# Even input projection as four pairs of column tiles, each a two by two blocked product with seven products

## The reference

```python
D_MODEL = 1024; SEQ = 1024
EV_IN = 4608     # 2*512 (q, k of A) + 2*1024 (v, gate of A) + 3*512 (q, k, v of B)
def _even_mixer(x, positions, w_in, w_out):
    hproj = x @ w_in                                   # (1024 x 1024) @ (1024 x 4608)
    qa, ka, va, ga, qb, kb, vb = [hproj[..., offs[i]:offs[i + 1]] for i in range(len(sizes))]
    qa = _rotary(_heads(qa, RET_HEADS), positions, RET_DK, RET_THETA)
    ...                                                # retention and dilated attention
    return jnp.concatenate([ya, yb], -1) @ w_out
```

## Time and profile before

| | |
|---|---|
| median of three runs (lowest to highest) | 3026.54 us (3023.1 to 3028.83) |
| span of the profiled execution | 3027.1 us |
| TensorE, VectorE, ScalarE, GpSimd busy | 94%, 61%, 40%, 11% of the span |
| the projection: first to last matmul | 13.8 to 408.2 us |
| its matmuls | 1728 |
| first work of the next stage (VectorE, L1367) | 418.0 us |

### The profile page before, as it was taken

One profiled execution on the slowest core, in us unless ns is written; L12 is line 12 of the kernel. 1 busy time (PEld: TensorE's weight loads), 2 busy tenths in 40 slices (PEclk: granted clock), 3 DMA queues, 4 the chain that ended last, 5 costly groups with the idle time before them and its releaser, 6 DMA issues. The chain is left out here.

```text
span 3027.1 us, 45981 instructions
## 1 busy us (share of the span) xinstructions
PE 2850.5 (94%) x17614; PEld 2398.2 (79%) x17614; DVE 1856.5 (61%) x2964; ACT 1209.1 (40%) x2127; POOL 334.0 (11%) x273
## 2 busy tenths in 40 slices
PE   8999977988989999999989989799988999999998
PEld 6888866877878888788877877689977888887886
DVE  4111125683789999836379882255538899997365
ACT  3211125762354444422346752355433444443222
POOL 0000036330000000000000001355410000000000
PEclk9999988998989999999989999899998999999999
DMA  4222234335322222264422432532033222224444
GB/s 169 88 95 95 83 142 127 94 96 181 97 92 84 84 84 84 100 210 145 163 98 84 159 99 79 171 105 95 17 133 105 85 84 84 84 84 158 158 153 142
DMA packets 150493, 339.70 MB, mean 112 GB/s; under 512 B 35952, under 2 KB 69936, under 8 KB 139696
## 3 DMA queue, kind: packets, MB, share of 16 engines
q1 hardware_dynamic: 120128, 299.52, 28.9%
q10 hardware_dynamic: 30192, 37.82, 3.6%
HBM read 252.17 MB, written 85.10 MB: 111 GB/s over the span
## 5 line engine op out<-in xcount | busy, mean ns | idle before, releaser
L308 PE MATMUL even_in_acc<-even_in_w_hi,even_x_hi 128*128 128x512 f32 x576 | 225.5, 391 | 13.8 <-DVE even_x_lo L266 13.8
L272 DVE TENSOR_TENSOR even_in_w_lo<-even_in_w_raw,even_in_w_hi 128x512 fp32r<-128x512 f32 x72 | 49.6, 691 | 292.3 <-ACT even_in_w_hi L229 292.3
L309 PE MATMUL even_in_acc<-even_in_w_lo,even_x_hi 128*128 128x512 f32 x576 | 225.2, 391 | 0.0
L310 PE MATMUL even_in_acc<-even_in_w_hi,even_x_lo 128*128 128x512 f32 x576 | 225.2, 391 | 0.0
L1034 DVE TENSOR_TENSOR ffn_a_lo<-ffn_a_raw,ffn_a_hi 128x512 fp32r<-128x512 f32 x80 | 55.3, 691 | 217.5 <-ACT ffn_a_hi L936 217.5
L936 ACT CAST ffn_a_hi<-ffn_a_raw 128x512 fp32r<-128x512 f32 x80 | 49.8, 623 | 307.1 <-PE ffn_down_acc L980 277.6
L1128 POOL TENSOR_TENSOR ffn_down_rstd<-ffn_down_rstd,ffn_down_power 128x1 f32<-128x1 f32 x16 | 15.0, 939 | 1368.4 <-DVE ffn_down_rstd L1063 1368.4
L308 PEld LDWEIGHTS even_in_acc<-even_in_w_hi,even_x_hi 128*128 128x128 f32 x576 | 108.8, 189 | 36.3 <-issue 13.8
L310 PEld LDWEIGHTS even_in_acc<-even_in_w_hi,even_x_lo 128*128 128x128 f32 x576 | 108.7, 189 | 22.9
L309 PEld LDWEIGHTS even_in_acc<-even_in_w_lo,even_x_hi 128*128 128x128 f32 x576 | 108.8, 189 | 22.5
L980 PE MATMUL ffn_down_acc<-two_hi,ffn_a_hi 128*128 128x512 f32 x352 | 109.2, 391 | 4.4 <-DVEq L1028 2.6
(11 more groups left out here) (571 smaller groups left out, 8288.9 us busy)
## 6 DMA issues: line engine op xcount, KB each, us to landing
ffn_w_raw<-in_ffn_up SPq DMA_DIRECT2D x42, 1024.0 KB, 4.8
ffn_down_w_raw<-in_ffn_down SPq DMA_DIRECT2D x82, 512.0 KB, 3.6
ffn_a_raw<-hidden SPq DMA_DIRECT2D x86, 256.0 KB, 3.7
even_in_w_raw<-in_ev_w_in SPq DMA_DIRECT2D x18, 1024.0 KB, 5.7
hp<-even_in_stage ACTq DMA_DIRECT2D x18, 1024.0 KB, 4.4
even_out_w_raw<-in_ev_w_out SPq DMA_DIRECT2D x24, 512.0 KB, 3.6
hidden<-even_mixed SPq DMA_DIRECT2D x22, 512.0 KB, 2.6
ffn_w_raw<-in_od_w_qkv SPq DMA_DIRECT2D x11, 1024.0 KB, 5.7
```

The source lines that it names most:

```text
L272: dve.tensor_tensor(at(w_lo, k), w_raw[:, k], f32(at(w_hi, k)), ALU.subtract).then_inc(lo_ready, 1)
L308: pe.matmul(acc[:, h, t], xhi[:, k, tok], at(w_hi, k), start=(k == 0), stop=False)
L309: pe.matmul(acc[:, h, t], xhi[:, k, tok], at(w_lo, k), start=False, stop=False)
L310: mm = pe.matmul(acc[:, h, t], xlo[:, k, tok], at(w_hi, k), start=False, stop=(k == KD - 1))
```

## The change

`project_tokens` is replaced for this projection by a new function, `project_pairs`. Tile 0 is computed as before (`plain`, 192 matmuls). Tiles 1 to 8 form four pairs (groups g). A pair is the product of x, cut into halves of tokens and halves of the contraction, with the two tiles, cut into the same halves of the contraction (`b11`, `b21` of the left tile, `b12`, `b22` of the right). It takes seven block products i = 0 to 6 in place of eight (`ORDER`), each of 4 token blocks x 4 chunks x 3 = 48 matmuls.

- Four sums and differences of blocks of x are made once, in `x_raw` (`sum_x`), and split; three go to `s_hi`, `s_lo`, one overwrites the quarter of `xhi`, `xlo` that is not used any more.
- Four sums and differences of weight blocks are made for each pair (`first_sums`, `third_sum`, `fourth_sum`), each 128x2048, in place.
- Products 0, 2, 4, 6 go to one set of four banks and 1, 3, 5 to the other. 2, 4 and 6 accumulate on what 0 left there, and 5 on 3; only 0, 1 and 3 open a bank. In between ScalarE copies the banks after 0, 2, 4 and 6 (`keep`), and VectorE adds the other set's banks to the copies after 1, 4 and 5 (`add`). `stage` and `u2` hold the copies, which then are the results.
- Weights are split four chunks at a time for the next product into two alternating places.
- Stores are issued from SyncE's queue, like the loads. `hp_stored` has three semaphores.
- The angles are reduced inside the first pair: the sine table during product 0, the cosine table during product 3.
- The loops are unrolled.

```diff
@@ -322,6 +322,343 @@
...
+def project_pairs(nc, name, xhi, xlo, w, n_tiles, out, x_dram, beside, stored):
+    KH = KD // 2
+    ORDER = 7
+    GROUPS = (n_tiles - 1) // 2
+    PLAIN = KD
+        s_hi, s_lo = (sc.sbuf(f"s_{part}", [P, 3, KH, HALF], F32R) for part in ("hi", "lo"))
+        w_hi, w_lo = (sc.sbuf(f"w_{part}", [P, 2, KH, NB], F32R) for part in ("hi", "lo"))
+        raw_left = sc.sbuf("raw_left", [P, 2, KH, NB])
+        raw_right = sc.sbuf("raw_right", [P, 2, KH, NB])
+        u2 = sc.sbuf("u2", [P, HALF_T, NB])
+        stage = sc.sbuf("stage", [P, HALF_T, NB])
+        acc = sc.psum("acc", [P, 2, HALF_T, NB])
...
+        b11, b21, b12, b22 = raw_left[:, 0], raw_left[:, 1], raw_right[:, 0], raw_right[:, 1]
+        toks = [slice(0, HALF), slice(HALF, SEQ)]
+        S1, S2, S4 = range(3)
+        def source(i):
+            return (b11, b21, b11, b12, b11, b21, b22)[i]
+        def operand(i, k):
+            if i in (2, 4, 6):
+                n = (S2, S1, S4)[i // 2 - 1]
+                return s_hi[:, n, k], s_lo[:, n, k]
+            kk, tok = {0: (k, 0), 1: (KH + k, 0), 3: (k, 1), 5: (KH + k, 1)}[i]
+            return xhi[:, kk, toks[tok]], xlo[:, kk, toks[tok]]
+        def banks(g, i):
+            return acc[:, (g + i) % 2]
...
+            sp.wait_ge(s_lo_ready, 4 * KH)
+            for s in range(2):
+                load_w(2, s, raw_right[:, s], 2 + s)
+            sp.wait_ge(plain_copied, 1)
+            sp.dma_start(rows(0, 0), stage[:]).then_inc(upper_stored, 16)
+            sp.wait_ge(plain_copied, 2)
+            sp.dma_start(rows(1, 0), u2[:]).then_inc(lower_stored, 16)
+            for g in range(GROUPS):
+                more = g + 1 < GROUPS
+                n0, n1 = 2 * g + 1, 2 * g + 2
+                split = PLAIN + KH * ORDER * g
+                sp.wait_ge(added, 3 * HALF_T * g + HALF_T)
+                sp.dma_start(rows(0, n0), stage[:]).then_inc(upper_stored, 16)
+                if more:
+                    sp.wait_ge(lo_ready, split + 4 * KH)
+                    load_w(n1 + 2, 0, b12, 2)
+                    sp.wait_ge(lo_ready, split + 5 * KH)
+                    load_w(n0 + 2, 0, b11, 0)
+                    sp.wait_ge(lo_ready, split + 6 * KH)
+                    load_w(n0 + 2, 1, b21, 1)
+                sp.wait_ge(added, 3 * HALF_T * g + 2 * HALF_T)
+                sp.dma_start(rows(1, n1), stage[:]).then_inc(lower_stored, 16)
+                if more:
+                    sp.wait_ge(lo_ready, split + 7 * KH)
+                    load_w(n1 + 2, 1, b22, 3)
+                sp.wait_ge(added, 3 * HALF_T * g + 3 * HALF_T)
+                sp.dma_start(rows(1, n0), u2[:]).then_inc(left_stored, 16)
+                sp.wait_ge(copied, 4 * HALF_T * (g + 1))
+                sp.dma_start(rows(0, n1), stage[:]).then_inc(upper_stored, 16)
...
+            def room(g, i, t):
+                if i == 0 and g == 0:
+                    pe.wait_ge(plain_copied, 1)
+                if i == 1 and g == 0:
+                    pe.wait_ge(plain_copied, 2)
+                if i == 0 and g > 0:
+                    pe.wait_ge(added, 3 * HALF_T * (g - 1) + 2 * HALF_T + t + 1)
+                if i == 1 and g > 0:
+                    pe.wait_ge(copied, 4 * HALF_T * (g - 1) + 3 * HALF_T + t + 1)
+                if i in (2, 4, 6):
+                    pe.wait_ge(copied, 4 * HALF_T * g + (i // 2 - 1) * HALF_T + t + 1)
+                if i in (3, 5):
+                    pe.wait_ge(added, 3 * HALF_T * g + (i // 2 - 1) * HALF_T + t + 1)
+            def product(g, i):
+                p = ORDER * g + i
+                opens = i in (0, 1, 3)
+                if g == 0 and i in (2, 3, 4, 6):
+                    pe.wait_ge(s_lo_ready, 4 * KH)
+                for t in range(HALF_T):
+                    room(g, i, t)
+                    tok = slice(t * P, (t + 1) * P)
+                    for k in range(KH):
+                        if t == 0:
+                            pe.wait_ge(lo_ready, PLAIN + KH * p + k + 1)
+                        hi, lo = operand(i, k)
+                        to, wh, wl = banks(g, i)[:, t], w_hi[:, p % 2, k], w_lo[:, p % 2, k]
+                        pe.matmul(to, hi[:, tok], wh, start=(opens and k == 0), stop=False, skip_group_check=not opens)
+                        pe.matmul(to, hi[:, tok], wl, start=False, stop=False, skip_group_check=not opens)
+                        mm = pe.matmul(to, lo[:, tok], wh, start=False, stop=(k == KH - 1), skip_group_check=not opens)
+                    mm.then_inc(prod_done, 1)
...
+            def split_hi(g, i):
+                p = ORDER * g + i
+                if p < 2:
+                    act.wait_ge(plain_done, 2 + p)
+                else:
+                    act.wait_ge(prod_done, HALF_T * (p - 1))
+                if i < 2:
+                    act.wait_ge(w_in[i], 16 * (g + 2))
+                elif i == 6:
+                    act.wait_ge(w_in[3], 16 * (g + 1))
+                else:
+                    act.wait_ge(w_summed, 4 * g + (2, 2, 4, 3)[i - 2])
+                for k in range(KH):
+                    act.copy(w_hi[:, p % 2, k], source(i)[:, k]).then_inc(hi_ready, 1)
+            def keep(g, i):
+                p = ORDER * g + i
+                if i == 0:
+                    act.wait_ge(upper_stored, 16 * (2 * g + 1))
+                if i == 2 and g == 0:
+                    act.wait_ge(lower_stored, 16)
+                if i == 2 and g > 0:
+                    act.wait_ge(left_stored, 16 * g)
+                if i == 4:
+                    act.wait_ge(upper_stored, 16 * (2 * g + 2))
+                if i == 6:
+                    act.wait_ge(lower_stored, 16 * (g + 2))
+                for t in range(HALF_T):
+                    act.wait_ge(prod_done, HALF_T * p + t + 1)
+                    act.copy((u2 if i == 2 else stage)[:, t], banks(g, i)[:, t]).then_inc(copied, 1)
...
+            act.wait_ge(plain_done, 1)
+            act.wait_ge(s_lo_ready, 3 * KH)
+            for k in range(KH):
+                split_sum(k, 3)
+            split_hi(0, 0)
+            act.wait_ge(s_lo_ready, 4 * KH)
+            act.copy(stage[:], acc[:, 0]).then_inc(plain_copied, 1)
+            act.wait_ge(plain_done, 3)
+            act.copy(u2[:], acc[:, 1]).then_inc(plain_copied, 1)
+            for g in range(GROUPS):
+                for i in range(ORDER):
+                    if i < ORDER - 1:
+                        split_hi(g, i + 1)
+                    elif g + 1 < GROUPS:
+                        split_hi(g + 1, 0)
+                    if i % 2 == 0:
+                        keep(g, i)
+                    if g == 0 and i == 1:
+                        other.run("act_sin", act)
+                    if g == 0 and i == 4:
+                        other.run("act_cos", act)
...
+            def first_sums(g):
+                for b in range(2, 4):
+                    dve.wait_ge(w_in[b], 16 * (g + 1))
+                dve.tensor_tensor(b12, b22, b12, ALU.subtract).then_inc(w_summed, 1)
+                dve.wait_ge(w_summed, 4 * g + 1)
+                dve.tensor_tensor(b11, b12, b11, ALU.add).then_inc(w_summed, 1)
+            def third_sum(g):
+                dve.wait_ge(w_summed, 4 * g + 2)
+                dve.tensor_tensor(b21, b21, b11, ALU.subtract).then_inc(w_summed, 1)
+            def fourth_sum(g):
+                dve.wait_ge(w_summed, 4 * g + 3)
+                dve.tensor_tensor(b11, b22, b11, ALU.subtract).then_inc(w_summed, 1)
+            def add(g, i):
+                p = ORDER * g + i
+                for t in range(HALF_T):
+                    if i == 1:
+                        kept, made, side = stage, ORDER * g + 1, 1
+                        dve.wait_ge(copied, 4 * HALF_T * g + t + 1)
+                    elif i == 4:
+                        kept, made, side = stage, ORDER * g + 3, 3
+                        dve.wait_ge(copied, 4 * HALF_T * g + 2 * HALF_T + t + 1)
+                    else:
+                        kept, made, side = u2, ORDER * g + 5, 5
+                        dve.wait_ge(copied, 4 * HALF_T * g + HALF_T + t + 1)
+                    dve.wait_ge(prod_done, HALF_T * made + t + 1)
+                    dve.tensor_tensor(kept[:, t], kept[:, t], banks(g, side)[:, t], ALU.add).then_inc(added, 1)
...
+            split_lo(0, 0)
+            for g in range(GROUPS):
+                for i in range(ORDER):
+                    if i < ORDER - 1:
+                        split_lo(g, i + 1)
+                    elif g + 1 < GROUPS:
+                        split_lo(g + 1, 0)
+                    if i == 0:
+                        first_sums(g)
+                    if i in (1, 4, 5):
+                        add(g, i)
+                    if i == 1:
+                        third_sum(g)
+                    if i == 2:
+                        fourth_sum(g)
+                    if g == 0 and i == 0:
+                        other.run("dve_sin", dve)
```

(42 more changed lines are left out.)

161 lines of the change are left out of this document (132 added, 29 removed).

## The result

The changed kernel took 2984.12 us (median of four runs, 2981.83 to 2985.66) against 3026.99 (four runs) for the kernel before: 42.9 us less, a ratio of 0.9856 with a 95% interval of 0.9842 to 0.987. The forecast was 2981.8 us.

A forecast was written before the change was run, and what follows sets the result against it. The prediction took TensorE's matmuls to bound the projection, busy 94% of the whole span. 3027.1 - 43.5 (fewer matmuls) - 1.2 (the end) = 2982.4 us, less 0.6 for the median: 2981.8 us; stated range 2976 to 2992, chance 0.65.

The forecast's parts named there:

- What bounds it: Projection: it lasts as long as its matmuls take; 1536 become 1344, 192 fewer at 0.2266 us, 43.5 us gained.
- The distance of matmuls: Projection matmuls, start to start: stays 0.2266 us despite the new order; bounds 0 to 1.4 us lost, taken 0.
- No waits in a pair: Steady pairs of the projection: splits, adds, copies and loads are ready before TensorE needs them; 0 us of wait.
- The first pair: First pair, with sums and angles: product 2's first chunk is 3.5 us ahead; 0, or up to 8.0 us once.
- The end: Handover to retention: one bank left to copy, 1.2 us gained; loads behind the last store between 0.9 gain and 1.3 loss, taken 0.
- the third rival: Handover to retention: loads queued behind the last store on one queue hold retention back 1.3 us, 2983.1 us; chance 0.12.
- the fourth: Projection products: weights split too late at every product, 2.8 us 28 times, 78 us less 44.7, 3060 us; chance 0.05.
- The tipping point: Fourth rival, projection products: a wait of 1.6 us per product, 44.7 / 28, decides whether the kernel gets slower.
- The fifth rival: Projection: micro-pauses at 112 block changes lower TensorE's clock; with 25% of matmuls slow 68 us, so 3050; chance 0.02.
- the prediction's sentence on that page: Fifth rival: by the skill's page on cycling through banks this stage would oscillate; by the trace it would not.
- The base: Whole kernel: the median of runs, 3026.54 us, was taken as 0.6 below the profiled span of 3027.1.

The follow-up runs named there:

- the execution with the eighth product: Product 3 of every pair computed twice, 192 matmuls more, all else as in the changed kernel: 3029.02 us (ten runs), ratio 1.0006 to the kernel before.

## Why the prediction was right, point by point

- **What bounds it.** Right: 192 matmuls fewer took the projection's end down by their time, and 192 put back restored it.
- **The distance of matmuls.** 0.2267 us within the pairs; waits that are already fulfilled, once in 3 matmuls, cost nothing that can be seen (bounds 0 to 1.4, taken 0).
- **No waits in a pair.** Right: no wait at any of 28 starts. Product 5 is the closest, and exposes 1.4 us if it is waited for as a whole.
- **The first pair.** VectorE's splits for product 2 started at 77.2 (77.9 forecast), with 3.5 us of cover (3.5).
- **The end.** Mis-sized term. 1.2 us of gain was taken; the first load did come 1.28 us sooner, but the loads took 6.3 to 7.2 us in place of 5.93, so 0 to 0.9 arrived. I had bounded this at a loss of 1.3 and taken 0; the execution with the eighth product (7.21, a handover of 9.61 as before the change) lost all of it. The reason given for the third rival, the order on one queue, is not borne out: on ScalarE's queue the loads took 6.24 and 6.90. The Trainium skill, "DMA: Bandwidth & Descriptors", section "Queues, rings and completion order", has the descriptors of one ring consumed in order. By that the loads would start behind the store's reads on SyncE's queue and not on ScalarE's; the traces do not show that difference. What is left open is why the kernel before needed only 5.93, with ScalarE's queue and the same 1 MB; there is a single trace of it.
- **Rivals.** The price of the fourth, 2.8 us a product, was too high for its mechanism: TensorE waits for the first chunk only, 1.5 us. That its total was near (70 us for 78) is luck: five waits of 3.8 us, of which the price knew nothing, and the slower matmuls behind all pauses, which no term of mine had, made up for it. The tipping point of 1.6 us a product would have been reached at 1.3 us of idle, since a short pause costs 0.29 us more than that. The fifth rival's clock loss was seen only behind pauses of 3.8 and 5.1 us, and the changed kernel has none. The Trainium skill, "TensorE: Matmul & The Clock Gate", section "A second HAM failure mode: psum-queue depth-cycling", has the loss of its bf16 kernel come from short idle times between groups of matmuls. Here 112 block changes within 304.64 us left no idle time and the clock at 1.00, so changing banks is not enough by itself; the prediction's sentence on that page read more into it.
- **The base.** The runs now list time and span together: 2983.13 and 2981.4 us, 1.7 apart. By that the profiled execution of before, with a span of 3027.1, took about 3028.8, 2.3 above the median, not 0.6. The difference forecast, 44.7 us, is unaffected. Measured were 42.9, and 46.6 when the unaltered kernel was run again: the traces' sum, 43.5 and 0 to 0.9, lies between, and the scatter of the later stages (14 us over twelve executions) is larger than any term that was missed. That the two profiled spans differ by 45.7 us, more than the forecast, is luck too: 0.5 of it is tile 0 and 1.4 the later stages.

## What to carry to other kernels

Where TensorE fills a stage without a wait, blocked products with seven for eight give one eighth of the paired part's matmuls times their distance, provided that every split, sum and handover is waited for in pieces and is ready earlier than it is used; work the cover out for each product start, since it is the smallest one (here 3.5 us, once) that decides. A pause of TensorE costs more than its idle time (here 0.3 us more at 1.5 us, 1.7 to 3.2 more at 3.8): price the slower matmuls behind it. Gains of 1 us that a trace shows need not show in the time of a kernel of 3000 us, and a single execution 7 us below its neighbours is scatter until it is repeated.

## What the runs showed that was not expected

- Behind a pause of 5.1 us nine matmuls stood 0.43 us apart, and behind five pauses of 3.8 us 6 to 14 of them. Behind pauses of 1.4 to 1.5 us none did: there the next twelve took 0.12 to 0.17 us too long, and the step to the first was 0.16 us more than the idle time shown.
- A load of 512 KB behind a 1 MB store was held back as much when the store was on the other engine's queue (6.24 and 6.90 us from the first load to VectorE's work, against 6.27 to 7.21); with only 256 KB of store beside it, it took 5.10 and 5.19. Its issue by SyncE alone lasted 0.93 us or more behind the 1 MB and 0.56 and 0.43 behind the 256 KB.
- The copy behind tile 0, whose matmuls no kernel here changes, started between 59.15 and 60.82 us: executions differ by over 1 us before the first pair begins.
